# Second block of a two-block layer: the order in which ScalarE copies turned probabilities and takes weights' high parts, the places of the recurrence's splits, and the order of half-array matmuls

## The reference, cut to what matters

```python
proj = einsum("bsd,de->bse", rms_norm_2(x, norm_g), w_in)          # D_IN columns
u = causal_depthwise_conv_2(proj[u], conv_w, conv_b)               # 4 taps
r, i = sigmoid(block_diag(u, w_a)), sigmoid(block_diag(u, w_x))    # 8 blocks of 128
log_a = -8 * r * softplus(-lam); a = exp(log_a)
h = scan(a, sqrt(1 - a**2) * (i * u)); y_rnn = h * silu(g_rnn)
scores = einsum("bnqkgd,bnjkd->bnkgqj", qb, kw) * scale            # 4 kv heads x 4 blocks, 256 keys each
p = exp(masked scores - m); probs = p / (sum(p) + exp(sink - m))
y_attn = einsum("bnkgqj,bnjkd->bnqkgd", probs, vw) * silu(g_attn)
merged = sigmoid(m_rnn) * (y_rnn @ w_rnn_out) + sigmoid(m_attn) * (y_attn @ w_attn_out)
x = x + merged @ w_o;  return rms_norm_2(x, final_norm_g)
```

## Time and profile before

| what | value |
|---|---|
| median of 3 runs (1372.62, 1372.66, 1375.75) | 1372.66 us |
| the profiled execution's own time | 1375.83 us |
| its span | 1374.1 us |
| mean granted TensorE clock | 0.993 |
| TensorE matmuls busy | 1344.3 us (98%) |
| VectorE busy | 837.7 us (61%) |
| ScalarE busy | 638.1 us (46%) |
| GpSimd busy | 60.9 us (4%) |

### The profile page before, as it was taken

One profiled execution on the slowest core, in us unless ns is written; L12 is line 12 of the kernel. 1 busy time (PEld: TensorE's weight loads), 2 busy tenths in 40 slices (PEclk: granted clock), 3 DMA queues, 4 the chain that ended last, 5 costly groups with the idle time before them and its releaser, 6 DMA issues.

```text
span 1374.1 us, 15781 instructions
## 1 busy us (share of the span) xinstructions
PE 1344.3 (98%) x6071; PEld 1076.1 (78%) x6071; DVE 837.7 (61%) x1115; ACT 638.1 (46%) x890; POOL 60.9 (4%) x62
## 2 busy tenths in 40 slices
PE   7999999999999999999999999999999999999998
PEld 6887666788878888888888888887876776778886
DVE  5456366699975667666667334635277787544444
ACT  6234766523353344333333233513378888644232
POOL 0000000000000120000000001200012220000000
PEclk9999999999999999999999999999999999999999
DMA  7421000142223232222332222432321122123311
GB/s 250 163 93 62 31 31 31 62 153 93 96 88 112 96 100 92 92 92 92 103 110 92 92 92 92 154 107 76 118 66 62 62 77 92 63 93 136 108 63 61
DMA packets 98283, 128.74 MB, mean 94 GB/s; under 512 B 2952, under 2 KB 80688, under 8 KB 97712
## 3 DMA queue, kind: packets, MB, share of 16 engines
q1 hardware_dynamic: 98208, 127.93, 28.1%
q10 hardware_dynamic: 16, 0.00, 0.0%
HBM read 121.63 MB, written 6.29 MB: 93 GB/s over the span
## 4 chain that ended last, share of the span: by engine, by line
PE 83%; DVE 8%; ACT 6%; issue 2%; DMA 1%; POOL 0%; SPq 0%; ACTq 0%; POOLq 0%; DVEq 0%
PE PS L1619 81%; PE PS L1686 1%; ACT WH L566 1%; DVE WL L986 1%; DVE SMALL L1467 1%; DVE CACC L1138 1%; DMA STAGE<-in_w_in 1%; ACT S2A L814 0%; DVE SPB L1203 0%; ACT PT L825 0%; ACT E L663 0%; ACT L663 0%; ACT E L662 0%; DVE S2A L1462 0%; ACT E L660 0%
## 5 line engine op out<-in xcount | busy, mean ns | idle before, releaser
L566 ACT ACTIVATE WH<-STAGE 128x1024 fp32r<-128x1024 f32 x214 | 225.7, 1057 | 491.3 <-PE PS L1619 476.7
L986 DVE TENSOR_TENSOR WL<-STAGE,WH 128x1024 fp32r<-128x1024 f32 x214 | 271.0, 1268 | 225.7 <-ACT WH L566 225.1
L1619 PE MATMUL PS<-XH,WH 128*128 128x512 f32 x960 | 382.8, 399 | 0.8 <-DVE ATT L1171 0.8
L1619 PE MATMUL PS<-XL,WH 128*128 128x512 f32 x960 | 375.0, 391 | 0.0
L1619 PE MATMUL PS<-XH,WL 128*128 128x512 f32 x960 | 374.9, 390 | 0.0
L1619 PEld LDWEIGHTS PS<-XH,WH 128*128 128x128 f32 x960 | 181.0, 189 | 45.0 <-issue 5.0
L1619 PEld LDWEIGHTS PS<-XL,WH 128*128 128x128 f32 x960 | 181.1, 189 | 38.3 <-issue 2.1
L1619 PEld LDWEIGHTS PS<-XH,WL 128*128 128x128 f32 x960 | 180.8, 188 | 38.2
L1619 PE MATMUL PS<-WH,XH 128*128 128x512 f32 x224 | 88.3, 394 | 0.5 <-DVE XL L1022 0.5
L1619 PE MATMUL PS<-WL,XH 128*128 128x512 f32 x224 | 87.4, 390 | 0.0
L1619 PE MATMUL PS<-WH,XL 128*128 128x512 f32 x224 | 87.2, 390 | 0.0
(11 more groups left out here) (299 smaller groups left out, 1927.5 us busy)
## 6 DMA issues: line engine op xcount, KB each, us to landing
STAGE<-in_w_in SPq DMA_DIRECT2D x52, 1024.0 KB, 5.0
STAGE<-in_w_up SPq DMA_DIRECT2D x22, 1024.0 KB, 5.1
STAGE<-in_w_down SPq DMA_DIRECT2D x11, 1024.0 KB, 4.9
STAGE<-in_w_out SPq DMA_DIRECT2D x4, 1024.0 KB, 5.0
STAGE<-in_w_rnn_out SPq DMA_DIRECT2D x4, 1024.0 KB, 5.0
STAGE<-in_w_attn_out SPq DMA_DIRECT2D x4, 1024.0 KB, 5.0
STAGE<-in_w_o SPq DMA_DIRECT2D x4, 1024.0 KB, 5.0
XTOK<-in_x SPq DMA_DIRECT2D x4, 512.0 KB, 6.7
```

The costliest lines, as they stand in the source:

```text
L566: act.activation(ring(WH, n), staged(n), ACT.Copy).then_inc(hi_done, 1)
L986: dve.tensor_tensor(ring(WL, n), staged(n), ring(WH, n).bitcast(F32), ALU.subtract)\
L1619: return pe.matmul(out_, lhsT, rhs, start=start, stop=stop, skip_group_check=True)
```

## The change

Three things are moved; no instruction is added or taken away.

1. ScalarE: at odd units, `window_pt` comes ahead of `hi(j+4)` (before, behind it).
2. The recurrence's splits: `rnn_hi` from units 18, 19, 20, 21 (3, 2, 2, 1 blocks) to units 19, 21, 22 (3, 3, 2 blocks); `rnn_low` from units 18, 19, 21, 22 to units 20, 22, 23.
3. TensorE: in `window_scores` and `window_values` the loop over the halves `par` becomes the inner one.

```diff
@@ ScalarE's loop
-                hi(U_GR + j + 4)
                 if j % 2 and 3 <= j < 35:
                     window_pt((j - 3) // 2)
+                hi(U_GR + j + 4)
@@
-                if j == 18:
-                    rnn_hi(range(3))
-                if j == 19:
-                    rnn_hi((3, 4))
-                if j == 20:
-                    rnn_hi((5, 6))
-                if j == 21:
-                    rnn_hi((7,))
+                if j in (19, 21, 22):
+                    rnn_hi({19: (0, 1, 2), 21: (3, 4, 5), 22: (6, 7)}[j])
@@ VectorE's loop
-                if j in (18, 19, 21, 22):
-                    rnn_low({18: (0, 1, 2), 19: (3, 4), 21: (5, 6), 22: (7,)}[j])
+                if j in (20, 22, 23):
+                    rnn_low({20: (0, 1, 2), 22: (3, 4, 5), 23: (6, 7)}[j])
@@ window_scores
-                for par in range(2):
-                    rows_ = slice(par * DH, (par + 1) * DH)
-                    for idx in range(2):
+                for idx in range(2):
+                    for par in range(2):
+                        rows_ = slice(par * DH, (par + 1) * DH)
@@ window_values
-                for par in range(2):
-                    for kb in kbs:
+                for kb in kbs:
+                    for par in range(2):
```

## The result

The change makes the kernel slower. The median is 1379.43 us (7 runs, 1377.33 to 1380.13), against 1373.18 for the kernel before (7 runs, 1372.62 to 1375.75); the ratio is 1.004, its 95% interval 1.0028 to 1.0052. The profiled execution took 1379.43 us itself, with a span of 1377.7 and a mean granted clock of 0.997. Against the profiled execution of before that is 3.6 us more, against the median 6.2. The profiled execution of before (1375.83) was a long one of its kernel: it has two stretches at half clock in this part, at units 6 and 22, where the one of after has one, and a stretch costs 1.7 us.

What follows compares the result with a forecast made beforehand. ScalarE and VectorE, waiting for each other in strict lists, bound TensorE: profiled 1375.83 + 0 (halves) + 2.0 (unit 24) = 1377.8 us, or 1379.5 with a low clock; range 1369.5 to 1381.5, the forecast's own 1376.8 to 1381.

Steps and rivals of the forecast that it cites:

- What bounds the kernel: Units 12 to 20: ScalarE and VectorE, each half idle, wait for each other and bound TensorE; PT waits worth at most 10.8 us.
- The chain through the low part and the square: ScalarE's high part, VectorE's low part, recurrence's square, ScalarE's first tap; makes ScalarE 1.0 us later at units 5, 9, 13, 17.
- The halves: TensorE's score and value matmuls in the second attention: the halves run side by side already, so alternating them gives 0.
- The page's rule: Matmuls start and end in program order; as a rival, alternating gives back 22 us over 28 blocks: 1355.8, chance 0.02.
- The swap: Odd units, PT ahead of the high part: PT 0.95 us earlier, high part 1.0 later, window 9's exponentials 4.0 late.
- the turn waits: TensorE's waits of the turn for scaled probabilities, forecast at units 7, 15 and 19 as a sign, without a size.
- the sum: Made against the profiled execution: 1375.83 + 0 + 2.0 = 1377.8 us, the 2.0 from unit 24.
- Unit 24: Block 6 is ready at 1179.7; TensorE waits 2 to 5 us and goes on 2.0 us later than before.
- the clock: If the clock falls in or behind unit 24's wait, 1.7 us more: 1379.5.

## Why the prediction was right

**What bounds the kernel: right.** Two engines that serve strict lists and wait for each other bound the third one. The chain through the low part and the square carried ScalarE's lateness, and moving the square (1370.80 without any other edit) shows it from the other side.

**The halves: right**, with 0 taken and +0.3 measured within an interval that spans 1. The reading that the halves ran side by side already was tested by the run on one half. The page's rule that I set against the row (the Trainium skill, TensorE: Matmul & The Clock Gate, part 3, the mechanism) would have made the old blocks about as long as those of one half, 1.99 us; the trace has 1.14.

**The swap: right in kind.** The first tap waits 2.26 us, forecast 2.3. At unit 8 L1466 takes 2.33, forecast 2.3, and the exponentials are 2.2 late, forecast 2.0. In window 9 they are 3.55 late, forecast 4.0. The way there was less exact: I had TensorE ahead by more than 1 us at unit 8, and it was ahead by 0.6 (scores at 1052.05 against 1052.68). Of the turn waits I named three, at units 7, 15 and 19; there is a fourth at unit 11. The waits for PT fell to 2.6 us, where I had said about 1. What I did not price is that the turn waits, 5.1 us, take back all that TensorE had gained. The forecast came out right all the same, because the sum was made at the one place where TensorE was to be held last, from ScalarE's side.

**Unit 24: right, and closer than the terms deserve.** Two windows took 1172.39 - 1145.96 = 26.4 us, forecast 26.2; TensorE goes on at 1179.73, forecast 1179.8 (2.0 later than before; measured 1.9). The wait is 3.36, within 2 to 5. That 1179.73 meets 1179.8 so well is in part luck: ScalarE was 0.45 us less late in window 9 than forecast, the two windows took 0.2 longer, the piece from window 11 to TensorE's going on took 0.1 longer (7.3 against 7.2), and the errors nearly cancel.

**The one step that was left out is the clock.** I put 1.7 us for a low clock in or behind this wait beside the sum and not in it: 1377.8, or 1379.5. It fell, and the profiled time and the median are both 1379.43. In the trace it costs 3.60 us at 0.53, 1.7 us. A wait of 3.4 us is longer than the 2.2 that had brought it down in the earlier trace rows, so by my own rows the higher number was the likelier one. In the two other traces that have a wait of 3.4 us there the clock fell as well.

**What stays open.** Up to unit 22 the lists leave 1.1 us unaccounted: before, 8.2 us of waits and 1.7 of low clock; after, 9.0 of waits and 0.2 less for the scores and values; yet both traces stand at 1163.56. Part of it is that a wait of the turn costs more than the list says. From the values of unit 10 to the turn of unit 11 there are 7.68 us before (1067.48 to 1075.16, no wait) and 9.03 after (1067.21 to 1076.24): 1.35 more, for a listed wait of 1.22. The turns of units 15 and 19, each from the values before it, show the same: 1.36 for 1.20 and 1.70 for 1.55. Four such waits make about 0.6 of the 1.1 us; the rest stays open.

## What to carry to other kernels

Where two engines serve fixed lists and wait for each other, look for the instruction that stands behind one that it doesn't need: here a square for the next tap stood behind a weight's low part that was wanted three units later, and two splits behind another. Such a position can cost at once (the square: 3.4 us in the kernel before), and its price grows when something upstream becomes late (the two splits: a wait of 2.3 us without the swap, 3.4 us and a low clock with it). Work out also how much room a mended place leaves; here it was 0.4 us. And a wait downstream of a point where two engines meet does not shrink when the work ahead of that point gets faster; only work between the meeting and the wait counts.

## What the runs showed of the hardware

- Half-array matmuls of 64x256 ran side by side whatever order the list had them in: blocks of 1.14 us in groups of four, 1.13 alternated, 1.99 when all used one half.
- The clock fell behind or in each of three waits of 3.4 us. Behind a wait of 2.2 us at unit 6 it fell in the kernel before, and behind one of the same length it did not where only the halves alternate. One stretch, near 124 us in the first layer, is in some of the traces and not in others, though that code is the same in all. Which stretches at half clock a single execution has thus varies from one to the next, and the forecast has to carry it as a chance.
- A low clock can change the order of events on other engines. In the trace where only the halves alternate it did not fall at unit 6, and GpSimd's product came 0.15 us ahead of VectorE's small step, which then took 2.27 us instead of 0.17; TensorE waited 0.90 us more at unit 10 and 0.5 more at unit 14. Of the 1.7 us that TensorE was ahead at the turn of unit 7, 0.24 were left at the values of unit 14 (1099.45 against 1099.69), and 0.14 of that was there at unit 0 already: the stretch at half clock had cost next to nothing in the end.
- GpSimd's product of 128x1024 elements holds a VectorE step on 128x4 elements until its end: 2.33 and 2.27 us, and where two products follow each other, two steps, 1.05 and 1.22 us. That fits the shared port pair of the Trainium skill (SBUF — State Buffer, SBUF: two separate sides), which one of the two engines has for a whole instruction.
